# Twenty weight slabs of a transformer trunk get their low part from an adding DMA instead of VectorE

## The reference, cut to what matters

```python
def conv_ffn(h, w_up, conv_w, conv_b, w_down):
    u = h @ w_up                                     # 2048 -> 2 x 5632
    up = jnp.pad(u, ((0, 0), (CONV_WIDTH - 1, 0), (0, 0)))
    u = conv_b + conv_w[0] * up[:, 0:S] + conv_w[1] * up[:, 1:S + 1] + conv_w[2] * up[:, 2:S + 2]
    g, val = u[..., :D_FF], u[..., D_FF:]
    return (jax.nn.silu(g) * val).astype(h.dtype) @ w_down      # 5632 -> 2048

for layer in range(2):
    x = x + rmsnorm(mixer(rmsnorm(x)))
    x = x + rmsnorm(memory_cross_attention(rmsnorm(x), mem))
    x = x + rmsnorm(conv_ffn(rmsnorm(x), ...))
```

## Time and profile before

| | |
|---|---|
| median of three runs | 2457.57 us (2455.85 to 2458.99) |
| span of the profiled execution | 2454.9 us |
| what lies around the span, against the median | 2.7 us |
| PE busy | 2436.8 us, 99% of the span |
| DVE busy | 1691.1 us, 69% |
| ACT busy | 1318.8 us, 54% |
| POOL busy | 55.6 us, 2% |
| DMA | 468.33 MB, mean 191 GB/s |

### The profile page before, as it was taken

One profiled execution on the slowest core, in us unless ns is written; L12 is line 12 of the kernel. 1 busy time (PEld: TensorE's weight loads), 2 busy tenths in 40 slices (PEclk: granted clock), 3 DMA queues, 4 the chain that ended last, 5 costly groups with the idle time before them and its releaser, 6 DMA issues.

```text
span 2454.9 us, 34925 instructions
## 1 busy us (share of the span) xinstructions
PE 2436.8 (99%) x12460; PEld 2077.0 (85%) x12460; DVE 1691.1 (69%) x2366; ACT 1318.8 (54%) x1897; POOL 55.6 (2%) x119
## 2 busy tenths in 40 slices
PE   9999999999999999999999999999999999999998
PEld 7888888888888888888888888888888888888887
DVE  6555666677777677778665466566777776778786
ACT  6345555665555555555454455556655555555553
POOL 0000000000000000000000002000000000000000
PEclk9999999999999999999999999999999999999999
DMA  8657455556656655656566675555566565656664
GB/s 288 195 185 250 148 165 172 185 165 196 186 183 192 193 181 187 218 193 215 182 192 183 200 213 168 171 176 172 180 187 199 174 194 188 193 181 208 203 215 155
DMA packets 247022, 468.33 MB, mean 191 GB/s; under 512 B 17520, under 2 KB 20736, under 8 KB 246912
## 3 DMA queue, kind: packets, MB, share of 16 engines
q1 hardware_dynamic: 234640, 447.83, 57.6%
q10 hardware_dynamic: 12272, 19.04, 2.4%
HBM read 464.69 MB, written 2.11 MB: 190 GB/s over the span
## 4 chain that ended last, share of the span: by engine, by line
PE 96%; DVE 2%; ACT 1%; DMA 0%; issue 0%; POOL 0%; DVEq 0%; SPq 0%; POOLq 0%; ACTq 0%
PE acc L1806 15%; PE acc L1785 10%; PE acc L1787 10%; PE acc L1786 10%; PE aux L1806 8%; PE acc L1814 8%; PE tp L1806 7%; PE acc L2211 5%; PE acc L2210 5%; PE acc L2209 5%; PE aux L1814 4%; PE tp L1814 4%; DVE w_lo L1072 1%; PE tp L2026 1%; PE acc L2047 1%
## 5 line engine op out<-in xcount | busy, mean ns | idle before, releaser
L1072 DVE TENSOR_TENSOR w_lo<-raw,w_hi 128x1024 fp32r<-128x1024 f32 x847 | 1020.6, 1222 | 548.0 <-ACT w_hi L501 544.5
L501 ACT ACTIVATE w_hi<-raw 128x1024 fp32r<-128x1024 f32 x847 | 868.5, 1055 | 386.3 <-PE acc L1787 127.6
L1806 PE MATMUL acc<-a_hl,w_hi 128*128 128x512 f32 x1568 | 486.4, 391 | 0.0
L1785 PE MATMUL acc<-w_hi,a_hl 128*128 128x512 f32 x988 | 391.4, 396 | 1.7 <-DVE a_hl L1100 1.6
L1787 PE MATMUL acc<-w_hi,a_hl 128*128 128x512 f32 x988 | 385.5, 390 | 0.0
L1786 PE MATMUL acc<-w_lo,a_hl 128*128 128x512 f32 x988 | 384.8, 389 | 0.0
L1806 PEld LDWEIGHTS acc<-a_hl,w_hi 128*128 128x128 f32 x1568 | 282.0, 189 | 47.3
L1814 PE MATMUL acc<-a_hl,w_lo 128*128 128x256 f32 x1568 | 315.0, 283 | 0.0
L1814 PEld LDWEIGHTS acc<-a_hl,w_lo 128*128 128x128 f32 x1568 | 257.0, 191 | 15.3
L1806 PE MATMUL aux<-a_hl,w_hi 128*128 128x512 f32 x832 | 256.9, 390 | 0.0
L1806 PE MATMUL tp<-a_hl,w_hi 128*128 128x512 f32 x736 | 227.3, 390 | 0.0
(11 more groups left out here) (263 smaller groups left out, 2506.7 us busy)
## 6 DMA issues: line engine op xcount, KB each, us to landing
raw<-in_w_up SPq DMA_DIRECT2D x352, 512.0 KB, 4.1
raw<-in_w_down SPq DMA_DIRECT2D x176, 512.0 KB, 4.7
raw<-in_w_in_c SPq DMA_DIRECT2D x96, 512.0 KB, 4.3
raw<-in_w_in_ab SPq DMA_DIRECT2D x95, 512.0 KB, 4.5
raw<-in_w_out_ab SPq DMA_DIRECT2D x32, 512.0 KB, 4.5
raw<-in_w_out_c SPq DMA_DIRECT2D x32, 512.0 KB, 4.3
raw<-in_w_mk SPq DMA_DIRECT2D x16, 512.0 KB, 4.1
raw<-in_w_mq SPq DMA_DIRECT2D x16, 512.0 KB, 4.2
```

Of the source, the lines that this page charges most:

```text
L501: act.activation(w_hi[:, s], raw[:, s], ACT.Copy).then_inc(hi_ready, 1)
L1072: dve.tensor_tensor(w_lo[:, s], raw[:, s], w_hi[:, s].bitcast(F32), ALU.subtract).then_inc(lo_ready, 1)
L1785: pe.matmul(o, hi[:, kt, rows], w_hi[:, slot, j, :], start=(kt == 0), stop=False)
L1806: last = pe.matmul(bank, w_hi[:, slot, j, f * P:(f + 1) * P], both, start=(kt == 0), stop=(kt == KT - 1))
```

## The change

In each layer the slab two behind an odd seven slab (the odd plain slab of the pair that follows it: 13, 19, 25, 31, 37 and 53, 59, 65, 71, 77) is taken from DVE. There are 20 of them in the two layers. For such a slab ACT does two copies: the usual one to `w_hi`, and one of `-raw` to `w_lo`, which rounds to the negative of `w_hi`. Then POOL issues a DMA that reads the raw weights from HBM again and adds them into `w_lo`, so that `w_lo` holds `raw - w_hi`.

```diff
+BY_DMA_AT = [k + 2 for k, (_, g, m) in enumerate(DOWN) if m is not None and g % 2]
+BY_DMA = [L * LAYER_SLABS + PHASE["down"] + k for L in range(LAYERS) for k in BY_DMA_AT]
+def lo_count(n, layer):
+
+    return n + 1 - (sum(m <= n for m in BY_DMA) if isinstance(n, int) else layer * len(BY_DMA_AT))
...
@@ block.sync @@
...
-                if not (isinstance(n, int) and n < RING):
-                    sp.wait_ge(lo_ready, n - (RING - 1))
+                if n - RING in BY_DMA if isinstance(n, int) else False:
+                    sp.wait_ge(hi_ready, n - (RING - 1))
+                    sp.wait_ge(low_negated, BY_DMA.index(n - RING) + 1)
+                elif not (isinstance(n, int) and n < RING):
+                    sp.wait_ge(lo_ready, lo_count(n - RING, layer[0]))
...
@@ block.scalar, the loop over down @@
                     q, c, m = DOWN[k + AHEAD]
-                    if m is None:
+                    if m is not None:
+                        seven_hi(k + AHEAD, q, c, m)
+                    elif k + AHEAD not in BY_DMA_AT:
                         ahead(n + k)
-                    else:
-                        seven_hi(k + AHEAD, q, c, m)
+                    if k + AHEAD + 1 in BY_DMA_AT:
+                        d = n + k + AHEAD + 1
+                        split(d, d % RING)
+                        act.activation(w_lo[:, d % RING], raw[:, d % RING], ACT.Copy, scale=-1.0).then_inc(low_negated, 1)
...
@@ block.vector, the loop over down @@
-                    if m is None:
+                    if m is not None:
+                        seven_lo(k + AHEAD, q, c, m)
+                    elif k + AHEAD not in BY_DMA_AT:
                         ahead(n + k)
-                    else:
-                        seven_lo(k + AHEAD, q, c, m)
...
@@ block.gpsimd @@
                 x_rstd(("ffn", L))
+                for k in BY_DMA_AT:
+                    n = L * LAYER_SLABS + PHASE["down"] + k
+                    d, (q, g, _) = BY_DMA.index(n), DOWN[k]
+                    pool.wait_ge(low_negated, d + 1)
+                    if d:
+                        pool.wait_ge(low_added, 16 * d)
+                    pool.dma_start(w_lo[:, n % RING],
+                                   w_down[L][q * SLAB_KT * P:(q + 1) * SLAB_KT * P, g * N:(g + 1) * N]
+                                   .rearrange("(j p) n -> p j n", p=P), accum_op=ALU.add).then_inc(low_added, 16)
                 y_rstd(("ffn", L))
...
@@ block.tensor @@
                 def plain(k, q, c):
 
-                    pe.wait_ge(lo_ready, n + k + 1)
+                    if n + k in BY_DMA:
+                        d = BY_DMA.index(n + k)
+                        pe.wait_ge(hi_ready, n + k + 1)
+                        pe.wait_ge(low_added, 16 * (d + 1))
+                    else:
+                        pe.wait_ge(lo_ready, lo_count(n + k, layer[0]))
```

More of the change, by code:

```diff
@@ L109 @@
 TOTAL_SLABS = LAYERS * LAYER_SLABS
+BY_DMA_AT = [k + 2 for k, (_, g, m) in enumerate(DOWN) if m is not None and g % 2]
+BY_DMA = [L * LAYER_SLABS + PHASE["down"] + k for L in range(LAYERS) for k in BY_DMA_AT]
+assert all(DOWN[k][2] is None and k + TAIL < len(DOWN) for k in BY_DMA_AT)
+def lo_count(n, layer):
+    return n + 1 - (sum(m <= n for m in BY_DMA) if isinstance(n, int) else layer * len(BY_DMA_AT))
 def build(nc, x, mem, positions, w_in_ab, w_out_ab, w_in_c, b_f, w_out_c,
@@ L239, in build @@
         slab_used = sem("slab_used")
+        low_negated = sem("low_negated")
+        low_added = sem("low_added")
         x_turned_landed = [sem(f"turned_x_{kt}_landed") for kt in range(SLAB_KT)]
@@ L399, in _ @@
         def _(sp):
+            layer = [0]
             def slab(n, s, src):
-                if not (isinstance(n, int) and n < RING):
-                    sp.wait_ge(lo_ready, n - (RING - 1))
+                if n - RING in BY_DMA if isinstance(n, int) else False:
[3 more added lines that the diff above has]
+                    sp.wait_ge(lo_ready, lo_count(n - RING, layer[0]))
                 sp.dma_start(raw[:, s], src.rearrange("(j p) n -> p j n", p=P)).then_inc(raw_landed[s], 16)
@@ L424, in _ @@
             for L in range(LAYERS):
+                layer[0] = L
                 n0 = L * LAYER_SLABS
@@ L1702, in two, with rstd @@
                 return lambda h=None: stats[:, row, k:k + 2] if h is None else stats[:, row, k + h:k + h + 1]
-            def rstd(layer, row, at, to, chain, done):
+            def rstd(c0, row, at, to, chain, done):
                 g = [two((row, at + 2 * c)) for c in range(D_GROUPS)]
@@ L1708, in rstd @@
                 pool.tensor_tensor(t[0](), g[0](), g[1](), ALU.add).then_inc(chain, 1)
-                pool.wait_ge(chain, 4 * layer + 1)
+                pool.wait_ge(chain, c0 + 1)
                 pool.tensor_tensor(t[1](), t[0](), g[2](), ALU.add).then_inc(chain, 1)
-                pool.wait_ge(chain, 4 * layer + 2)
+                pool.wait_ge(chain, c0 + 2)
                 pool.tensor_tensor(t[0](), t[1](), g[3](), ALU.add).then_inc(chain, 1)
-                pool.wait_ge(chain, 4 * layer + 3)
+                pool.wait_ge(chain, c0 + 3)
                 pool.tensor_scalar(t[2](), t[0](), EPS, None, ALU.add).then_inc(chain, 1)
-                pool.wait_ge(chain, 4 * layer + 4)
+                pool.wait_ge(chain, c0 + 4)
                 pool.tensor_tensor(two((1, to))(), t[2](), minus_half[:], ALU.pow).then_inc(done, 1)
@@ L1739, in x_rstd @@
                 pool.wait_ge(*SV(sub, "x_sq", HALF * 4))
-                rstd(sub[1], 0, 0, 0, S(sub, "xc"), S(sub, "rstd"))
+                rstd((8 if sub[0] == "mix" else 4) * sub[1], 0, 0, 0, S(sub, "xc"), S(sub, "rstd"))
             def fox_masks(L):
@@ L1758, in _ @@
                     pool.wait_ge(sem("mem_sq"), HALF * 4)
-                    rstd(0, 0, 8, 2, sem("mc"), sem("m_rstd"))
+                    rstd(4, 0, 8, 2, S(("mix", L), "xc"), sem("m_rstd"))
                 if L:
@@ L1789, in slab @@
             def slab(n, slot, par, k0, kts, hi, lo, ready=None):
-                pe.wait_ge(lo_ready, n + 1)
+                pe.wait_ge(lo_ready, lo_count(n, layer[0]))
                 for h in range(HALF):
@@ L1869, in start @@
                     for s in range(1, GS):
-                        pe.wait_ge(lo_ready, n + s + 1)
+                        pe.wait_ge(lo_ready, lo_count(n + s, layer[0]))
                         for h in range(HALF):
@@ L1901, in tail @@
                                 y_free(sub, g)
-                            pe.wait_ge(lo_ready, e - TAIL + k + 1)
+                            pe.wait_ge(lo_ready, lo_count(e - TAIL + k, layer[0]))
                         last = half_slab(h, (e - TAIL + k) % RING, g % 2, SLAB_KT * s, kts, hi, lo)
```

## The result

The changed kernel takes 2585.52 us (median of four runs, 2583.17 to 2587.81), against 2456.8 us for the kernel before in the same job: a ratio of 1.0524, 95% interval 1.0512 to 1.0537. The forecast of 2498.6 us had the sign and the place right, and a third of the size. The loss is 128.7 us, not 41.

A forecast was written before the change was run, and what follows sets the result against it. PE was taken as the bound, busy 2436.8 of 2454.9 us. 2454.9 + 2.7 around it + 41 of PE waits - 0 for DVE's relief = 2498.6 us; range 2455.5 to 2552, likeliest case 2478 to 2534.

The forecast's parts named there:

- What bounds: Whole program: PE is the bound, busy 2436.8 of 2454.9 us, with one hole of 0.3 us in down.
- DVE's and ACT's terms, SP's and POOL's order: In down: DVE losing 24.4 us of splits, ACT gaining 19 us of copies, SP's shifted loads and POOL's issues count zero.
- The lead of 5.2 us: Slab 25 of layer 0: time from the negated copy's end, 1051.25, to PE wanting the low part, 1056.46.
- The length of the transfer: POOL's adding transfer, issue to landing: 3.5 + 1.54 + 1.54 + 0.6 = 7.2 us, so PE waits 2.0 us, 20 times.
- The base and POOL together: Parts of the transfer's length: 3.5 us as the fastest plain load, plus 0.6 us for POOL's small operation.
- the second read: Part of the transfer's length: 1.54 us because an adding transfer must read what it adds to.
- the sharing: Part of the transfer's length: 1.54 us because one plain load shares the DMA engines with it.
- What a wait costs: PE before the twenty slabs: each wait of 2.0 us adds in full, 40 us, plus 1 us for the first slabs.
- PE's clock stays at its full level: Expected sign in the profile after, for PE in down: granted clock unchanged despite 20 waits of about 2 us.
- The slow adder: Rival: DMA sum or POOL's command writing is slow; at 11.0 us per transfer 116 us lost, 2574; chance 0.15.
- The loads that are pushed back do not make a second wait: Plain loads in down, delayed by up to 1.54 us, are covered by 2 us of slack from PE's wait.
- The two rules of the Trainium skill: For the transfer: a reducing DMA's second read nearly halves the rate; a GpSimd-issued 512 KB DMA takes an estimated 3.2 us.

## Why the prediction was wrong

- *What bounds.* Right: PE, with 0.3 us of holes in down. The kernel without transfers shows it: 2457.46 against 2456.89 us.
- *DVE's and ACT's terms, SP's and POOL's order.* Right, all zero. The copies alone cost nothing, and DVE's waits for the output norms from POOL are as before (3.0 us where they were 3.2).
- *The lead of 5.2 us.* Right. 0.45 us of handing over (0.31 from the copy to POOL's issue, 0.14 from the landing to PE) were not in my sum.
- *The length of the transfer*, the step that failed first. I took 7.2 us; it is 9.0. The base and POOL together were 3.5 + 0.6 and measure 4.2; the second read was 1.54, and the adding measures 1.5 (some of it may be POOL's longer issue). The term that was mis-sized is the sharing: I let one plain load's 1.54 us pass in between, and it costs 3.3 us in the kernel (9.0 - 5.7) and 3.9 beside a full stream. My explanation is that a transfer with more engine time is also interleaved with others for longer; the kernel with nothing but transfers fits it, with 3.9 us for the adding transfer and 2.3 for the plain one. PE's wait is then 9.0 + 0.45 - 5.2 = 4.25 us, 85 by twenty, and 83.4 was measured.
- *What a wait costs*, the step that was missing. I counted a wait of PE at its own length. It costs more than that, since the clock is granted at 0.50 behind it: the slab takes 4.2 to 5.3 us in place of 2.72 in all twenty cases. With a few matmuls of the next slab and the 3 us named above that is 45.5 us in all. "PE's clock stays at its full level" was the wrong sentence. 83.1 + 45.5 = 128.6.
- *The slow adder.* This rival came nearest in time (2574), but not in its mechanism: the adder is as fast as reckoned when alone (3.5 + 1.54 + 0.6 = 5.6, measured 5.7). That its 11.0 us lands near the measured time is luck, since it has too long a transfer and no clock.
- *"The loads that are pushed back do not make a second wait".* True in the changed kernel, where PE's waits give them room, but only there. With PE waiting for none of the transfers, 30 us are lost at and behind the seven pairs with adding transfers, and 11 with plain ones. The second bound was hidden behind the first.
- *The two rules of the Trainium skill.* The reducing DMA's second read, as "Collectives: The Full Stack" (The bandwidth ceiling) of the Trainium skill has it, agrees with the 1.5 us here. The estimate of 3.2 us from the fit in "DMA: Bandwidth & Descriptors" (Anatomy of one DMA, SWDGE path) of the Trainium skill for a transfer issued by GpSimd is below the 4.2 us measured alone, and far below the 6.5 beside a stream.

What stays open: why some slabs behind a wait lose the clock and others keep it. In the kernel with plain transfers it fell behind waits of 2.06 and 2.10 us and stayed behind 2.25, 2.33 and 2.41; in the one with half of each slab added it fell behind 1.87 us and stayed behind 3.24. So the length of the wait alone does not decide it, and no run here isolates what does.

## What to carry to other kernels

Before moving work off an engine, look whether anyone waits for that engine; at 99% on PE the best that relief can bring is the sum of PE's holes. Price a new transfer by its engine time (bytes, and reads of the destination too) among the transfers that are in flight at that moment, and compare the whole path from producer to consumer with the lead. And where PE would wait, add to the wait what the matmuls behind it lose in clock, which here was half as much again.

## What the runs showed of the hardware

- An adding transfer of 512 KB by POOL: 5.7 us alone, 9.6 beside a stream of plain loads; a plain one 4.2 and 6.5. In the changed kernel a packet of it holds a DMA engine for 2.5% of 16 x 2583.5 us over 5440 packets = 0.19 us, against 0.097 for SP's plain loads. In the kernel with plain transfers it is 1.5% of 16 x 2508.3 us = 0.11 us for POOL's.
- POOL is busy issuing for 1.20 us per adding transfer, 0.72 per plain one, and 0.85 when it adds half the rows.
- In the changed kernel, behind all twenty waits of 3.1 to 5.9 us, PE ran at a granted clock of 0.50 for seven to fourteen matmuls. Behind waits of 1.8 to 3.3 us in the other kernels it did or did not (1.87 lost it, 3.24 kept it), and behind shorter ones it kept 1.00. Filling the pause with eighteen matmuls that add zero kept it at 1.00 and made the kernel 39 us faster.
